# First layer of a two-layer decoder step: cached memory scores in column groups, layer norm beside the memory blocks, output products between attention items

## What is computed

```python
h = _rms(x, P['norm_mix'][l])
a, g, mq = jnp.split(h @ P['w_in_a'][l], [C_A, 2 * C_A], axis=-1)
c, st = _causal_dwconv(a * jax.nn.sigmoid(g), conv_a_prev[l], P['conv_a_w'][l], P['conv_a_b'][l])
c = jax.nn.silu(_layernorm(c, P['ln_a_g'][l], P['ln_a_b'][l]))
...
mq = _rms(mq.reshape(b, t, MEM_HEADS, MEM_HD), P['mem_q_norm'][l])
m = _mem_attend(mq, mem_k[l], mem_v[l])
x = x + jnp.concatenate([c, m], axis=-1) @ w_out
...
x = x + (jax.nn.gelu(gate) * val) @ P['w_down'][l]
```

## Time and profile before

| | |
|---|---|
| median of 3 runs | 1452.77 us (1451.54 to 1454.21) |
| the profiled execution | 1450.41 us, span 1448.7 us |
| TensorE busy | 1378.8 us, 95% of the span |
| TensorE weight loads | 1284.8 us |
| VectorE busy | 861.9 us, 59% |
| ScalarE busy | 516.2 us, 36% |
| GpSimd busy | 188.7 us, 13% |
| chain that ended last | TensorE 79%, VectorE 11%, ScalarE 4% |

### The profile page before, as it was taken

How to read it: one execution, slowest core, us unless ns; L and a number is a source line. 1 busy time by engine, 2 the same in 40 slices (tenths; PEclk the granted TensorE clock), 3 DMA queues, 4 the chain that set the end, 5 groups by cost and what they waited for, 6 DMA issues and landing times.

```text
span 1448.7 us, 28167 instructions
## 1 busy us (share of the span) xinstructions
PE 1378.8 (95%) x11024; PEld 1284.8 (89%) x11024; DVE 861.9 (59%) x1721; ACT 516.2 (36%) x856; POOL 188.7 (13%) x245
## 2 busy tenths in 40 slices
PE   5999988999999999999999898898999999999997
PEld 5777767999999999999888776778999999999997
DVE  5444567566635663567776677775766436644652
ACT  4422356344312221224543444443534212221232
POOL 3323412220000000002102322320200000000001
PEclk8999999999999999999999999999999999999999
DMA  8344452243333333322323433332432333333222
GB/s 242 101 108 106 109 170 63 81 139 87 87 88 89 88 87 89 89 77 85 86 83 88 124 103 114 108 101 64 117 88 87 87 88 88 87 88 88 84 76 68
DMA packets 227822, 141.51 MB, mean 98 GB/s; under 512 B 9275, under 2 KB 217872, under 8 KB 227671
## 3 DMA queue, kind: packets, MB, share of 16 engines
q1 hardware_dynamic: 219295, 117.96, 28.8%
q0 software_dynamic: 7840, 21.89, 5.1%
q10 hardware_dynamic: 584, 0.23, 0.1%
HBM read 126.19 MB, written 7.85 MB: 93 GB/s over the span
## 4 chain that ended last, share of the span: by engine, by line
PE 79%; DVE 11%; ACT 4%; issue 2%; SPq 2%; DMA 1%; ACTq 1%; DVEq 0%
PE acc L549 64%; PE acc L764 3%; PE psT L706 3%; SPq L452 2%; DVE softmax_stats L2136 1%; ACT exps L1528 1%; PE acc L561 1%; DVE w_lo L1667 1%; ACT w_hi L1207 1%; PE psX L561 1%; DVE xa_lo L1712 1%; DVE psX L2134 1%; PE psT L1017 1%; DVE root_row L1700 1%; DVE x_resid L2019 0%
## 5 line engine op out<-in xcount | busy, mean ns | idle before, releaser
L549 PE MATMUL acc<-xa_hi,w_hi 128*128 128x272 f32 x1760 | 372.8, 293 | 6.9 <-DVE w_lo L1667 6.9
L549 PE MATMUL acc<-xa_hi,w_lo 128*128 128x272 f32 x1760 | 365.1, 289 | 0.0
L549 PE MATMUL acc<-xa_lo,w_hi 128*128 128x272 f32 x1760 | 363.9, 288 | 0.0
L1207 ACT ACTIVATE w_hi<-w_raw 128x1024 fp32r<-128x1024 f32 (+1 forms) x202 | 206.8, 1024 | 378.3 <-PE acc L549 346.4
L1667 DVE TENSOR_TENSOR w_lo<-w_raw,w_hi 128x1024 fp32r<-128x1024 f32 (+1 forms) x202 | 240.0, 1188 | 94.0 <-ACT w_hi L1207 92.5
L549 PEld LDWEIGHTS acc<-xa_hi,w_hi 128*128 128x128 f32 x1760 | 278.0, 189 | 17.9 <-issue 9.0
L549 PEld LDWEIGHTS acc<-xa_lo,w_hi 128*128 128x128 f32 x1760 | 277.5, 189 | 0.0
L549 PEld LDWEIGHTS acc<-xa_hi,w_lo 128*128 128x128 f32 x1760 | 275.9, 189 | 0.0
L549 PE MATMUL acc<-xb_hi,w_hi 128*128 128x272 f32 x896 | 194.0, 298 | 2.0 <-DVE xb_lo L2082 2.0
L549 PE MATMUL acc<-xb_hi,w_lo 128*128 128x272 f32 x896 | 185.3, 288 | 0.0
L549 PE MATMUL acc<-xb_lo,w_hi 128*128 128x272 f32 x896 | 184.7, 288 | 0.0
(11 more groups left out here) (338 smaller groups left out, 1723.7 us busy)
## 6 DMA issues: line engine op xcount, KB each, us to landing
w_raw<-in_w_up SPq DMA_DIRECT2D x88, 512.0 KB, 3.8
w_raw<-in_w_down SPq DMA_DIRECT2D x32, 512.0 KB, 3.9
w_raw<-in_w_in_a SPq DMA_DIRECT2D x14, 512.0 KB, 4.3
glu_shifted<-glu_rows SPq DMA_DIRECT2D x96, 67.5 KB, 2.0
w_raw<-in_w_down SPq DMA_DIRECT2D x16, 384.0 KB, 3.4
w_raw<-in_w_kv SPq DMA_DIRECT2D x12, 512.0 KB, 3.9
k_pages<-in_cache_k POOLq DMA_DIRECT2D x96, 64.0 KB, 2.3
v_pages<-in_cache_v SPq DMA_DIRECT2D x96, 64.0 KB, 2.1
```

Of the source, the lines that this page charges most:

```text
L549: last = nc.tensor.matmul(acc[slot][:, c, 0:n], w, x[:, k, c * n:(c + 1) * n], start=(k == 0 and q == 0), stop=(k == kb - 1 and q == 2))
L1207: nc.scalar.activation(whi[:, slot % 2, 0:n], wraw[:, slot, 0:n], ACT.Copy).then_inc(w_hi_ready, 1)
```

## The change

The sample parts of layer 0's memory attention take the form of the second layer: cached keys of four sequences are kept turned, and their scores are computed in four groups of 32 columns; value products are done in halves of 64 columns. The first four sequences' keys are turned beside the memory blocks, which needs the cached keys sooner: GpSimd issues their loads after the last input block. The layer norm (centring, squares, sums, root, swish, rounding) runs beside the memory blocks and before the first item; GpSimd centres three of the six chunks. Block rows 0 to 4 of the first two output blocks stand between items 2 to 6, row 5 after the samples' value product, rows 6 and 7 at the end. The second layer's key norm and value turn, the convolution's tail (now prompt and samples in one, 62 rows) and the memory keys' output turns go into the last down group of layer 0's feed-forward, and their stores to the SyncE queue behind that layer's weights. The gated unit writes the samples' new columns directly.

The diff, cut to its core (most removed lines are left out; they are those of the functions named above):

```diff
+        aturns = [("KM", b_) for b_ in range(4)]
+        for m in range(8):
+            if m < 4:
+                aturns.append(("KM", 4 + m))
+            if m == 4:
+                aturns.append(("GM", 1))
+            if m == 6:
+                aturns.append(("XT", 0))
+            aturns.append(("T", m))
+        aturns.append(("XO", 0))
...
                             load(i * 4 + s, src, kb=n)
                 if l == 0:
+                    sp.wait_ge(mv_c, 2)
+                    sp.dma_start(a["p_mem_v"][1][0].rearrange("(m p) h d -> p m (h d)", p=P), memv[:, 1, :, :]
+                                 ).then_inc(st_mk, 16)
+                    sp.wait_ge(ct_c, 2)
+                    sp.dma_start(a["p_conv_a"][0][0], ctail[0:TAPS - 1, :]).then_inc(st_cs, 16)
+                    sp.dma_start(a["s_conv_a"][0][:, TAPS - 1 - DS:, :], ctail[TAPS - 1:NTAIL, :]).then_inc(st_cs, 16)
+                    sp.wait_ge(mk_c, 2)
+                    for x in range(2):
+                        sp.dma_start(a["p_mem_k"][x][0].rearrange("(m p) h d -> p m (h d)", p=P), mkn[:, x, :, :]
+                                     ).then_inc(st_mk, 16)
...
-                if (s, k) == (S_MEM + 1, 4):
-                    pe.wait_ge(taps_summed, CC - 1)
-                    conv_tail()
-                if (s, k) == (S_MEM + 3, 5):
-                    pe.wait_ge(ln_m, 1)
+                if (s, k) == (S_MEM + 1, 2):
+                    a_turn_memory(0)
+                if (s, k) == (S_MEM + 2, 1):
+                    pe.wait_ge(aturn_taken, 1)
                     memory_key_squares(0)
-                if (s, k) == (S_MEM + 4, 4):
-                    pe.wait_ge(taps_summed, CC)
-                    memory_values_turned(0)
-                if (s, k) == (S_MEM + 5, 6):
-                    pe.wait_ge(ct_c, 3)
-                    memory_keys_out(0)
-                if (s, k) == (S_MEM + 6, 5):
-                    pe.wait_ge(mem_var, 1)
-                    memory_key_squares(1)
-                if (s, k) == (S_MEM + 2, 6):
-                    pe.wait_ge(ct_c, 3)
+                if (s, k) == (S_MEM + 2, 3):
                     pe.wait_ge(conv_total, CC - 1)
                     for c in range(2):
                         last = nc.tensor.matmul(psX[:, c, 0:HT], ones[:, :], csum[:, c * HT:(c + 1) * HT],
                                                 start=True, stop=True)
                     last.then_inc(ln_mean, 1)
+                if (s, k) == (S_MEM + 2, 5):
+                    a_turn_memory(1)
+                if (s, k) == (S_MEM + 3, 2):
+                    a_turn_memory(2)
+                if (s, k) == (S_MEM + 3, 6):
+                    a_turn_memory(3)
+                if (s, k) == (S_MEM + 4, 1):
+                    pe.wait_ge(taps_summed, CC)
+                    memory_values_turned(0)
+                if (s, k) == (S_MEM + 4, 3):
+                    a_memory_scores(0)
+                if (s, k) == (S_MEM + 4, 5):
+                    pe.wait_ge(sq_used, SQ["ln"] + 3)
+                    pe.wait_ge(as_c, 1)
+                    for c in range(2):
+                        nc.tensor.matmul(psX[:, c, 0:HT], ones[:, :], total[:, c * HT:(c + 1) * HT], start=True, stop=False)
+                    square_sum(SQ["ln"] + 3, psX, ones[:, :], first=False, final=False)
+                if (s, k) == (S_MEM + 4, 7):
+                    square_sum(SQ["ln"] + 4, psX, ones[:, :], first=False, final=False)
+                if (s, k) == (S_MEM + 5, 1):
+                    square_sum(SQ["ln"] + 5, psX, ones[:, :], first=False)
...
+            def a_scores(m):
+                c, tb = divmod(m, QB)
+                if m == 0:
+                    pe.wait_ge(qk_done, 4)
+                    pe.wait_ge(turned, RT["ln"] + 1)
+                else:
+                    pe.wait_ge(ma_exp, m)
+                for x in range(2):
+                    r = slice(x * MHD, (x + 1) * MHD)
+                    last = nc.tensor.matmul(psX[:, x, 0:MEM], mq[r, c, tb * P:(tb + 1) * P], memk[r, 0, c, :],
+                                            start=True, stop=True)
+                last.then_inc(ma_S, 1)
...
+            def a_turn(m):
+                pe.wait_ge(ma_p, m + 1)
+                aturn_free("T", m)
+                for x in range(4):
+                    last = nc.tensor.transpose(psT[:, 0, x * P:(x + 1) * P], et[:, m % 2, x * P:(x + 1) * P], ident)
+                last.then_inc(aturn_full, 1)
...
+                for mb in range(MB):
+                    for x in range(2):
+                        last = nc.tensor.matmul(psT[x * MHD:(x + 1) * MHD, 1, 0:P],
+                                                memv[:, 0, mb, c * P + x * MHD:c * P + (x + 1) * MHD],
+                                                pTt[:, 2 * x + mb, :], start=(mb == 0), stop=(mb == MB - 1))
+                last.then_inc(ma_pv, 1)
...
+            def a_memory_scores(b2):
+                if b2 == 0:
+                    pe.wait_ge(qm_ready, 1)
+                    pe.wait_ge(ln_m, 1)
+                else:
+                    aturn_free("GM", 1)
+                pe.wait_ge(aturn_taken, aturn_at("KM", 4 * b2 + 3) + 1)
+                bank = (psX[:, 1, MEM:2 * MEM], psT[:, 0, 0:MEM])[b2]
+                for c in range(MC):
+                    for j in range(4):
+                        last = nc.tensor.matmul(bank[j * NSA:(j + 1) * NSA, :], qm[:, c, 4 * b2 + j, :],
+                                                kTm[:, j, c * MEM:(c + 1) * MEM], start=(c == 0), stop=(c == MC - 1))
+                last.then_inc((as_S, aturn_full)[b2], 1)
...
+            for m in range(8):
+                if m < 7:
+                    a_scores(m + 1)
+                if m < 4:
+                    a_turn_memory(4 + m)
+                if m == 4:
+                    a_memory_scores(1)
+                if m == 6:
+                    a_memory_turn()
+                if m:
+                    a_weighted(m - 1)
+                if m >= 2 and m < 7:
+                    out_parts((0, 1), (m - 2,))
+                a_turn(m)
+            a_memory_weighted()
+            out_parts((0, 1), (CC - 1,))
+            a_weighted(7)
+            a_memory_turn_back()
+            out_parts((0, 1), range(CC, KD))
             def out_section():
-                out_parts((0, 1), range(KD))
                 for m in range(2, KD):
                     out_parts((m,), range(KD))
...
+                        if (m, k) == (0, 3):
+                            memory_key_squares(1)
+                        if (m, k) == (0, 5):
+                            memory_values_turned(1)
+                        if (m, k) == (2, 4):
+                            conv_tail()
+                        if (m, k) == (3, 2):
+                            memory_keys_out(0)
+                        if (m, k) == (3, 4):
+                            memory_keys_out(1)
                     if k == 3 and m:
                         after_chunk(l, m - 1)
...
+            def ln_square(j):
+                if j < 3:
+                    act.wait_ge(ln_c, j + 1)
+                else:
+                    act.wait_ge(ln_cp, j - 2)
+                square(convt[:, j, :])
...
+            split_hi(16)
+            a_turned_memory(0)
+            split_hi(17)
+            act.wait_ge(acc_free, 16)
+            square(qf[:, 0, 0:2 * MEM], 2 * MEM)
+            root(2 * MEM)
...
+            a_turned_memory(1)
+            split_hi(18)
+            ln_square(0)
+            ln_square(3)
+            a_turned_memory(2)
+            split_hi(19)
+            ln_square(1)
+            ln_square(4)
+            a_turned_memory(3)
+            ln_square(2)
+            memory_values(0)
+            split_hi(20)
+            ln_square(5)
+            root(T)
+            split_hi(21)
+            swish(0)
+            swish(1)
+            ln_high(0)
+            split_hi(22)
+            swish(2)
+            ln_high(1)
+            swish(3)
+            ln_high(2)
+            split_hi(23)
+            swish(4)
+            ln_high(3)
+            swish(5)
+            ln_high(4)
+            ln_high(5)
+            a_exponents(0)
+            for m in range(8):
+                if m < 4:
+                    a_turned_memory(4 + m)
+                if m == 5:
+                    a_memory_exponents()
+                if m < 7:
+                    a_exponents(m + 1)
+                if m == 6:
+                    a_memory_turned()
+                a_turned_probs(m)
+            a_mix()
...
                         split_hi(s + 2)
+                        if l == 0 and m == 1:
+                            root(2 * MEM)
...
+                dve.wait_ge(qm_zero, 1)
+                dve.wait_ge(qk_done, 2)
+                for c in range(MC):
+                    for x in range(2):
+                        r = slice(x * MHD, (x + 1) * MHD)
+                        at = (2 * c + x) * DS
```

(82 more changed lines are left out.)

595 lines of the change are left out of this document (242 added, 353 removed).

## The result

The changed kernel takes 1458.49 us (median of 6 runs, 1457.6 to 1458.92) against 1452.51 for the kernel before in the same comparison: a ratio of 1.0041, 95% interval 1.0031 to 1.0051. It is 6.0 us slower; 4.6 faster was forecast, and 1452.5 was the range's end. The profiled execution took 1458.73 us (span 1457.1, mean clock 0.985), 8.3 more than that of before.

A forecast was written before the change was run, and what follows sets the result against it. TensorE was taken as the bound outside the items' stretch, where a chain of waits runs through VectorE. To the first output block -7.8 us, feed-forward +3.2: 1452.77 - 4.6 = 1448.2 us; 8-in-10 range 1442.0 to 1452.5.

The forecast's parts named there:

- The walk of the memory blocks: Memory blocks 16 to 19 beside the layer norm, timed block by block: block 18 ends at 193.1, block 19 at 196.9.
- the wait of 1.7 us for the spread queries: Block 18: TensorE arrives at 186.4, VectorE finishes the spread at 188.1, so the grouped scores wait 1.7 us.
- the lock: GpSimd's five additions beside VectorE among the memory blocks, sharing a port pair: 1.5 us taken, bounds nothing and 5.2.
- Rival B: Among the memory blocks, the port lock makes GpSimd's additions cost 5.2 us instead of 1.5: 1451.9, no change; chance 0.17.
- the clock: After the longer TensorE hole, items 0 and 1 run at the lower clock level: 1.6 us, bounds 0 and 4.
- From scores to exponents: ScalarE's tail from the first item's scores to the end of its exponents: 9.0 us, ending at 212.5.
- The items: Memory attention: items 0 to 2 some 2.7 us each, items 2 and 3 with an output row 3.62; sum 24.9.
- Rival C: Memory attention items serialize, period 5.4 us instead of 3.6: 1459.8; gain gone from period 4.3; chance 0.1.
- The first output block: End of the first output block: 247.1 + 1.6 + 1.5 = 250.2, against 258.0 before, so -7.8 us.
- The feed-forward: Last down group of layer 0's feed-forward takes key squares, value turn, tail transposes and key turns: +3.2 us.
- Rival D: Grouped cached scores: the four column groups run one after another, so grouping brings nothing; excluded, no chance given.
- a first exponent after 217: Sign that the forecast is wrong through the port lock; first exponents were expected near 212 to 214.

The follow-up runs named there:

- the kernel with an early spread: Changed kernel with VectorE's spread of the memory queries moved to right behind the key variance, ahead of the first centring: 1454.89 us, ratio 1.0013.
- the filled kernel: Changed kernel with unread matmuls filling TensorE's waits, 18 ahead of the grouped scores and 32 behind the first item's scores: 1454.99 us, ratio 1.0018.
- the reordered kernel: Changed kernel with the layer norm off GpSimd, query spread and centrings earlier on VectorE, cached-key copy ahead of squares on ScalarE: 1451.15 us, ratio 0.9998.

## Why the prediction was wrong

*The walk of the memory blocks failed, in the step for block 18: the wait of 1.7 us for the spread queries, with the lock priced beside it.* It had the grouped scores wait 1.7 us for the spread, and start 27.3 us behind the last convolution product; they waited 4.71 and started at 32.4. The list of what stood ahead of the spread was right. Each length on it was one of an undisturbed VectorE, and GpSimd's overlap, counted apart at 1.5 us "as most of VectorE's work there has slack", was 4.5 us in just the instructions of that list and 0.3 in the centring ahead of it. The error was to price the lock for the stage and the wait for the queue, and not the one inside the other: between the centring and the spread VectorE had no slack at all. Rival B named the mechanism and its size (5.2 us); it did not name the spread, where the stretched instructions add up, and held the blocks' slack against itself. Its 1451.9 was passed all the same, by the clock and the items below.

*What a wait brings with it was not in the sum.* Behind the hole of 4.71 us the clock fell, and block 18 cost 2.4 us more than in the kernel with an early spread, 2.9 more than in the one with a busy TensorE (6.3 us from the grouped scores to the last square sum). I had charged the clock only at the items (1.6; the filled kernel shows 2.9 over three of them). With 5.1 for the later grouped scores and 2.4 to 2.9 for the clock, 7.5 to 8.0 of the 8.6 us by which the first item's scores were late are accounted for. All of it had gathered by the end of block 19; the two blocks behind took 6.4 us where the walk had 6.6. The remaining 0.6 to 1.1 stay open. Part of the 2.4 is chance: two other profiles with the same hole show 1.3 and 1.8.

*From scores to exponents*: right. From the first item's scores to the end of its exponents, ScalarE's tail took 8.8 us (213.12 to 221.95) against 9.0.

*The items*: too short. The first two ran near 4 us at half clock, not 2.7. At full clock an item was 4.08 and not 3.62: the row 1.70 (1.51 was reckoned from the average of a long run), the key turn 0.65 (0.44), and ScalarE's copy of the turned probabilities (0.60) in the place of the scores (0.64). From the first exponents to the end of the first output block it was 40.3 us against 36.2 with the clock's 1.6. Rival C's place was right, that turn, copy and row are one chain in the single bank; its threshold of 4.3 us was passed only by the item with the grouped scores (4.48), and the mean of the six periods is 4.1, so it is not C that decided. That the measured 1458.49 lies near C's 1459.8 is chance.

*The first output block*: 250.2 was forecast, 89.4 us behind the last convolution product; measured 262.24, 100.5 behind. The 11.1 are 7.0 from the blocks (8.6 less the 1.5 booked, and ScalarE's 0.1 to 0.2) and 4.1 from the items.

*The gap at the first output block* stayed, 2.43 us (262.24 to 264.67), as said. *The cached keys' loads* cost nothing, as said. *The feed-forward*: +3.2 for +3.2, right in its parts too; it is paid because TensorE is the limit there, and moving two of its four parts into a wait gave 1.7 us of it back. *Rival D* stays excluded: the grouped scores take 1.07 us at full clock. *What was left of the gain*: in the reordered kernel the norm's queues hold nothing up ahead of the grouped scores, and still the restart is only 4.1 us earlier than before (95.6 against 99.7), where 7.8 was forecast. From the first item's scores on it takes the same 51.6 us as the changed kernel, so the shortfall is mostly the items', and 3.2 of the 4.1 go back in the feed-forward: level with before.

The forecast named "a first exponent after 217" as the sign against it. It came at 220.92. The Trainium skill, "SBUF — State Buffer", section "SBUF: two separate sides", says that of a GpSimd instruction and a VectorE instruction with two inputs in SBUF, whichever starts first has the shared port pair for its whole length and the other blocks fully. The rows above agree: 1.1 us more for a VectorE instruction that starts behind an addition of 1.34, and nothing more for the one that started first. By that rule the upper end of 5.2 was the term to take, and 4.8 was measured.

## What to carry to other kernels

Price an engine's overlap with a neighbour inside the queue that feeds the next wait, not for the stage: a long list ahead of one small instruction has no slack, however idle its engine is on average. Look first at the order in such a queue; moving eight copies up into a wait gave 3.6 us, and taking GpSimd's work over to VectorE gave 2.8 us (three centrings), lost 3.1 or gave 2.7 (all of it), by where in VectorE's queue it was put. Work put "between" the steps of a chain costs what the chain no longer waits for, so take the period that the change leaves (2.9 us here), not the one it found (3.5).

## What the runs showed of the hardware

An addition of 128 x 544 on GpSimd took 1.34 us alone and 1.82 to 2.31 beside VectorE; VectorE's difference of 128 x 1024 took 2.38 beside it against 1.22, and eight copies of 64 x 16 took 2.22 against 1.08, though each has a single input. TensorE at the lower clock level took 1.23 us for four scores against 0.70 and 1.93 for sixteen grouped ones against 1.07; filling matmuls in the hole ahead kept it at the upper one. Behind the same hole of 4.71 us the same stretch took 8.1, 8.6 and 9.2 us in three executions, 6.3 with the hole filled. The start of the last convolution product moved by 3.3 us among thirteen profiles of programs that are alike up to there (160.3 to 163.6), more than most single edits were worth: it had to be taken out before two profiles could be compared.
